# First two experts' token lists from 16 columns of marks, and the first three tiles' result rows gathered in two passes

## What is computed

```python
def hierarchical_moe(xn, w_rg, b_rg, w_re, b_re, w_g, w_u, w_d):
    ...
    g_sel = jnp.argmax(g_logits, axis=-1)
    ...
    top_v, top_i = lax.top_k(e_in, TOP_K)
    top_p = jax.nn.softmax(top_v, axis=-1) * g_w
    expert_idx = (g_sel[:, None] * EXPERTS_PER_GROUP + top_i).reshape(-1)
    ...
    def expert_block(args):
        xb, e = args
        hb = jax.nn.silu(xb @ w_g[e]) * (xb @ w_u[e])
        return hb @ w_d[e]
    ...
    out = jnp.zeros((t, d), xt.dtype).at[token_idx[order]].add(y)
```

## Time and profile before

| | us |
|---|---|
| median of 3 runs | 2050.01 (2047.39 to 2053.05) |
| profiled execution | 2050.37 |
| its span | 2048.6 |
| PE busy | 1976.5 (96%) |
| DVE busy | 992.1 (48%) |
| ACT busy | 558.7 (27%) |
| POOL busy | 416.3 (20%) |

### The profile page before, as it was taken

The page is one execution under the profiler, slowest core; times in us unless marked ns, Lnnn a source line. Parts: engine busy times, 40 slices in busy tenths (PEclk is TensorE's granted clock), DMA queues, the critical chain, the costliest instruction groups (busy, mean ns, idle before and its releaser), DMA issues.

```text
span 2048.6 us, 38041 instructions
## 1 busy us (share of the span) xinstructions
PE 1976.5 (96%) x15458; PEld 1121.0 (55%) x15458; DVE 992.1 (48%) x1739; ACT 558.7 (27%) x1011; POOL 416.3 (20%) x381
## 2 busy tenths in 40 slices
PE   7999999999899999999999999999899999999997
PEld 6476655756434445454445554565566666666653
DVE  3434553455576753586656765444632222222225
ACT  4123231433576221143123421143011111111113
POOL 0304333325252004003000243000011111111113
PEclk9999999999999999999999999999999999999999
DMA  9221230212525012980030411202699999999997
GB/s 398 86 83 37 68 108 26 98 30 84 180 103 175 31 65 74 244 198 1 0 123 11 144 42 56 91 32 75 250 373 399 404 405 412 407 402 413 405 411 273
DMA packets 114572, 369.74 MB, mean 180 GB/s; under 512 B 22920, under 2 KB 58152, under 8 KB 91696
## 3 DMA queue, kind: packets, MB, share of 16 engines
q1 hardware_dynamic: 67520, 280.37, 35.1%
q0 software_dynamic: 20976, 69.23, 11.1%
q10 hardware_dynamic: 25984, 18.91, 2.9%
HBM read 319.17 MB, written 58.07 MB: 184 GB/s over the span
## 4 chain that ended last, share of the span: by engine, by line
PE 86%; DVE 7%; ACT 3%; issue 2%; POOL 1%; DMA 1%; DVEq 0%; ACTq 0%; POOLq 0%; SPq 0%; PEldq 0%
PE bank L760 19%; PE bank L1641 16%; PE bank L753 13%; PE bank L970 9%; PE bank L1651 8%; PE bank L996 2%; PE bank L1056 2%; ACT work L1751 2%; PE bank L1171 1%; PE bank L1632 1%; DVE work L2293 1%; PE bank L828 1%; DVE O L2293 1%; PE bank L1394 1%; PE bank L1164 1%
## 5 line engine op out<-in xcount | busy, mean ns | idle before, releaser
L1751 ACT ACTIVATE work<-bank 128x512 f32<-128x512 f32 (+5 forms) x246 | 123.0, 519 | 327.8 <-PE bank L760 96.1
L1751 ACT ACTIVATE work<-work 128x1024 f32<-128x1024 f32 (+5 forms) x200 | 158.8, 805 | 170.2 <-DVEq L158 114.6
L1751 ACT ACTIVATE HT<-bank 64x256 f32<-64x256 f32 (+1 forms) x150 | 67.8, 452 | 468.1 <-PE bank L1641 303.4
L753 PE MATMUL bank<-slots,HT 128*128 128x512 f32 (+2 forms) x576 | 184.1, 475 | 2.0 <-ACT HT L1751 1.5
L1641 PE MATMUL bank<-slots,HT 128*32 128x256 f32 x3136 | 172.4, 379 | 2.2 <-DVE HT L3152 1.3
L1641 PE MATMUL bank<-work,HT 128*32 128x256 f32 x3072 | 168.7, 379 | 0.0
L3158 DVE TENSOR_TENSOR HT<-HT,bank 64x256 f32<-64x256 f32 x97 | 41.2, 424 | 259.7 <-ACT HT L1751 254.9
L3277 POOL TENSOR_TENSOR work<-work 128x1024 f32<-128x1024 f32 (+1 forms) x64 | 111.9, 1748 | 239.7 <-DVEq L158 160.7
L1641 PEld LDWEIGHTS bank<-slots,HT 128*32 128x32 f32 x3136 | 103.0, 110 | 68.5 <-DMA slots<-in_w_e_up_dram 1.4
L753 PEld LDWEIGHTS bank<-slots,HT 128*128 128x128 f32 x576 | 98.3, 190 | 76.6 <-issue 71.2
L1641 PEld LDWEIGHTS bank<-work,HT 128*32 128x32 f32 x3072 | 101.2, 110 | 64.6
(11 more groups left out here) (356 smaller groups left out, 3114.7 us busy)
## 6 DMA issues: line engine op xcount, KB each, us to landing
slots<-in_w_e_gate_dram SPq DMA_DIRECT2D x34, 1024.0 KB, 9.6
slots<-in_w_e_up_dram SPq DMA_DIRECT2D x34, 1024.0 KB, 12.2
slots<-in_w_e_down_dram SPq DMA_DIRECT2D x17, 2048.0 KB
work<-in_w_e_gate_dram SPq DMA_DIRECT2D x32, 1024.0 KB
work<-in_w_e_up_dram SPq DMA_DIRECT2D x32, 1024.0 KB
work<-in_w_e_down_dram SPq DMA_DIRECT2D x16, 2048.0 KB
y_of_slot<-masks POOLq DMA_DIRECT2D x1, 19712.0 KB, 105.7
slots<-in_w_in_dram SPq DMA_DIRECT2D x8, 2048.0 KB, 8.9
```

Of the source, the lines that this page charges most:

```text
L753: ins = pe.matmul(bank, lhsT, rhs, start=(n == 0), stop=(n == len(pairs) - 1))
L1751: return act.activation(o, i, f, bias=bias, scale=scale, **more)
```

## The change

It does two things. First, the lists of experts 0 and 1 no longer come from the marks of all experts. DVE writes FIRST_MARKS, 16 columns (two experts by eight tiles), scans and hands them to PE ahead of A2. PE makes their ranks alone, then each expert's list in a bank of its own; `index[0]` goes to POOL while index 1 is still open. DVE hears POOL's issue of gather 0, then scans A2; GT, the one-hots OH, PICKED and RANK_OF come after index 1, and the block arithmetic is now `blocks_and_rows()`, behind the first `block_ready`. Dummy products: 3, 1 and 2 where there were 3, 3 and 5, and the last two stand ahead of `emptied()` rather than behind it. Second, POOL gathers the result rows of tiles 0, 1 and 2 twice: a first time ahead of the spare blocks, with all numbers of spare rows out of bounds and so skipped, and a second time after `moe_over` with `spare_id`, in which the regular rows are out of bounds. The readers wait for four transfers of such a tile.

```diff
+        TWICE = 3
         combined = [*((s, 32) for s in dma_in), *((sem(f"combine_rows{i}"), 0) for i in range(4, NT))]
         out_sem = x_in
         YG = [work[:, i * D:(i + 1) * D] for i in range(16)]
...
 
+            def ranks(marks, upto, n):
+
+                bank = ringV.open(pe)[:, 0:n]
+                pe.matmul(bank, const("negtri"), marks, start=True, stop=False)
+                ringV.close(pe.matmul(bank, const("ones"), upto, start=False, stop=True))
+
             hear("dve")
-            n = NT * EXPERTS
-            bank = ringV.open(pe)[:, 0:n]
-            pe.matmul(bank, const("negtri"), A2, start=True, stop=False)
-            ringV.close(pe.matmul(bank, const("ones"), UPTO, start=False, stop=True))
+            ranks(FIRST_MARKS, FIRST_UPTO, 2 * NT)
+            idle_products(banks[0], 1)
+            for e in range(2):
+                bank = ringV.open(pe)[0:CAP, 0:1]
+                for i in range(NT):
+                    at = e * NT + i
+                    if at % MARKED == 0:
+                        pe.wait_ge(rows_marked, at // MARKED + 1)
+                    ins = pe.matmul(bank, ROWS[:, at, :], FIRST_TOKENS[:, at:at + 1], start=(i == 0), stop=(i == NT - 1))
+                ringV.close(ins)
+            hear("dve")
+            ranks(A2, UPTO, NT * EXPERTS)
             bank = ringV.open(pe)[:, 0:EXPERTS]
             ringV.close(pe.matmul(bank, const("ones"), cut(UPTO, EXPERTS)[:, :, NT - 1], start=True, stop=True))
-            idle_products(banks[0], 3)
-            bank = ringV.open(pe)[0:CAP, 0:2]
-            for at in range(2 * NT):
-                if at % MARKED == 0:
-                    pe.wait_ge(rows_marked, at // MARKED + 1)
-                ins = pe.matmul(bank, ROWS[:, at, :], FIRST_TOKENS[:, at, :], start=(at == 0), stop=(at == 2 * NT - 1))
-            ringV.close(ins)
 
             def turn_block(x, last):
                 for half, bank in enumerate(TURN_BANKS):
@@ -1653,8 +1663,8 @@
                                             start=(f == 0), stop=(f == DE // P - 1))
                 ins.then_inc(full, 1)
 
+            idle_products(banks[0], 2)
             emptied()
-            idle_products(banks[0], 5)
             pe.wait_ge(rows_gathered[0], 16)
             turn_block(0, tokens_turned)
             def list_products():
@@ -1721,7 +1731,7 @@
                 residual(n)
             pe.wait_ge(diags_ready, 1)
             for n, i in enumerate(SUMMED):
-                pe.wait_ge(combined[i][0], combined[i][1] + 32)
+                pe.wait_ge(combined[i][0], combined[i][1] + (64 if i < TWICE else 32))
                 for half, bank in enumerate(sum_banks(n)):
                     for x in range(2):
...
@@ -3065,9 +3075,8 @@
             g = LG[:, :, 0:GROUPS]
             e = LG[:, :, GROUPS:].rearrange("p i (g x) -> p i g x", g=GROUPS)
             by_group = "p (i x g) -> p i g x"
-            reduce(R1, g, ALU.max)
-            first_of(OHG, g, R1, GROUPS, RG)
-            tt(GT, g, wide(R1, GROUPS), ALU.subtract)
+            reduce(R3, g, ALU.max)
+            first_of(OHG, g, R3, GROUPS, RG)
             tt(CHOSEN.rearrange(by_group, i=NT, g=GROUPS), e, bcast(OHG.unsqueeze(3), [P, NT, GROUPS, PER_GROUP]), ALU.mult)
             best = cut(BEST, NT)
             reduce(BEST, CHOSEN.rearrange("p (a g) -> p a g", g=GROUPS), ALU.add)
@@ -3077,34 +3086,52 @@
             reduce(R2, best, ALU.max)
             first_of(FIRST[1], best, R2, PER_GROUP, INDEX[:, NT:])
             tt(FIRST[2], FIRST[0], FIRST[1], ALU.add)
+            first = "p (x i) -> p i x"
+            tt(FIRST_MARKS.rearrange(first, x=2), bcast(OHG[:, :, 0:1], [P, NT, 2]), FIRST[2][:, :, 0:2], ALU.mult)
+            line(dve.tensor_tensor_scan(FIRST_UPTO, OF_EXPERT[:, 0:2 * NT], FIRST_MARKS, 0.0, ALU.mult, ALU.add))
+            tell("pe")
+            tt(cut(FIRST_TOKENS, 2), cut(FIRST_MARKS, 2), bcast(const("token").unsqueeze(1), [P, 2, NT]), ALU.mult)
             shape = [P, NT, GROUPS, PER_GROUP]
             tt(A2.rearrange("p (g x i) -> p i g x", g=GROUPS, i=NT), bcast(OHG.unsqueeze(3), shape),
                bcast(FIRST[2].unsqueeze(2), shape), ALU.mult)
+
+            def mark_rows(at, of):
+
+                some, shape = slice(at, at + MARKED), [P, MARKED, CAP]
+                dve.tensor_tensor(ROWS[:, some, :], bcast(const("slot_of_row").unsqueeze(1), shape),
+                                  bcast(of[:, some].unsqueeze(2), shape), ALU.is_equal).then_inc(rows_marked, 1)
+
+            empty(lambda b: dve.tensor_copy(FIRST_RANKS, b[:, 0:2 * NT]))
+            hear("pool")
+            for at in range(0, 2 * NT, MARKED):
+                mark_rows(at, FIRST_RANKS)
+
+            def first_index(x):
+
+                bank = ringV.take(dve)
+                line(dve.tensor_scalar(EMPTY[0:CAP, x:x + 1], bank[0:CAP, 0:1], 0.0, 2.0 * T, ALU.is_equal, ALU.mult))
+                line(dve.scalar_tensor_tensor(out=index[x][0:CAP, :], in0=bank[0:CAP, 0:1], scalar=-1.0,
+                                              in1=EMPTY[0:CAP, x:x + 1], op0=ALU.add, op1=ALU.add), ringV.free)
+                tell("pool")
+
+            first_index(0)
+            hear("pool")
             line(dve.tensor_tensor_scan(UPTO, OF_EXPERT, A2, 0.0, ALU.mult, ALU.add))
             tell("pe")
+            tt(GT, g, wide(R3, GROUPS), ALU.subtract)
+            first_index(1)
             tt(R3, R2, R1, ALU.subtract)
             tell("act")
             for x in range(2):
                 tt(OH[:, x * NT:(x + 1) * NT, :].rearrange("p i (g x) -> p i g x", g=GROUPS), bcast(OHG.unsqueeze(3), shape),
                    bcast(FIRST[x].unsqueeze(2), shape), ALU.mult)
-            ts(RG, RG, float(PER_GROUP), 1024.0 * (PER_GROUP + 1), ALU.mult, ALU.add)
-            tt(cut(INDEX, 2), cut(INDEX, 2), bcast(RG.unsqueeze(1), [P, 2, NT]), ALU.add)
-
-            tt(FIRST_TOKENS.rearrange("p (x i) e -> p x i e", x=2), OH.rearrange("p (x i) e -> p x i e", x=2)[:, :, :, 0:2],
-               bcast(const("token").unsqueeze(1).unsqueeze(3), [P, 2, NT, 2]), ALU.mult)
             shape = [P, 2, NT, EXPERTS]
             four = "p (x i) e -> p x i e"
             empty(lambda b: dve.tensor_tensor(
                 PICKED.rearrange(four, x=2), OH.rearrange(four, x=2),
                 bcast(b[:, 0:NT * EXPERTS].rearrange("p (e i) -> p i e", i=NT).unsqueeze(1), shape), ALU.mult))
             reduce(RANK_OF, PICKED, ALU.add)
-            hear("pool")
-
-            def mark_rows(at, of):
-
-                some, shape = slice(at, at + MARKED), [P, MARKED, CAP]
-                dve.tensor_tensor(ROWS[:, some, :], bcast(const("slot_of_row").unsqueeze(1), shape),
-                                  bcast(of[:, some].unsqueeze(2), shape), ALU.is_equal).then_inc(rows_marked, 1)
+            empty(lambda b: dve.tensor_scalar(SPN, b[:, 0:EXPERTS], 1.0 / TG, BELOW - (CAP + 1 - TG) / TG, ALU.mult, ALU.add))
 
             def mark(at):
 
@@ -3114,34 +3141,27 @@
                 tt(TOKENS[:, some, :], TOKENS[:, some, :], bcast(const("token")[:, i:i + MARKED].unsqueeze(2), shape), ALU.mult)
                 mark_rows(at, ROW_OF)
 
-            for at in range(0, 2 * NT, MARKED):
-                mark_rows(at, RANK_OF)
-            empty(lambda b: dve.tensor_scalar(SPN, b[:, 0:EXPERTS], 1.0 / TG, BELOW - (CAP + 1 - TG) / TG, ALU.mult, ALU.add))
-            bank = ringV.take(dve)
-            line(dve.tensor_scalar(EMPTY[0:CAP, 0:2], bank[0:CAP, 0:2], 0.0, 2.0 * T, ALU.is_equal, ALU.mult))
-            for x in range(2):
-                line(dve.scalar_tensor_tensor(out=index[x][0:CAP, :], in0=bank[0:CAP, x:x + 1], scalar=-1.0,
-                                              in1=EMPTY[0:CAP, x:x + 1], op0=ALU.add, op1=ALU.add), ringV.free if x else None)
-            tell("pool")
-            hear("pool")
-
...
+            def blocks_and_rows():
+
+                ts(RG, RG, float(PER_GROUP), 1024.0 * (PER_GROUP + 1), ALU.mult, ALU.add)
+                tt(cut(INDEX, 2), cut(INDEX, 2), bcast(RG.unsqueeze(1), [P, 2, NT]), ALU.add)
...
@@ -3190,6 +3210,8 @@
                 ts(BEYOND, BLOCK_OF, -float(EXPERTS), 0.0, ALU.add, ALU.max)
                 stt(SLOT, BEYOND, -float(CAP - TG), SLOT, ALU.mult, ALU.add)
                 copy(slot_id[:, :], SLOT)
+                ts(BEYOND, SLOT, float(EXPERTS * CAP), BEYOND_Y, ALU.is_lt, ALU.mult)
+                line(dve.tensor_tensor(spare_id[:, :], SLOT, BEYOND, ALU.add))
                 ts(PIECES, ASSIGNED, const("slot_of_piece"), BEYOND_Y, ALU.is_le, ALU.mult)
                 line(dve.tensor_tensor(piece_list[:, :], PIECES, const("piece_of_y"), ALU.add))
                 dve.sem_inc(routed, 1)
@@ -3216,6 +3238,7 @@
             line(dve.memset(token_list[:, :], 0))
             dve.wait_ge(tokens_turned, 1)
             block_ready(tokens_ready)
+            blocks_and_rows()
             expert(0, 0, first=True)
             expert(0, 1, second=True)
```

(21 more changed lines are left out.)

40 lines of the change are left out of this document (21 added, 19 removed).

## The result

The changed kernel takes 2062.89 us (median of 5 runs, 2058.05 to 2063.33) against 2050.01 (5 runs too, 2047.39 to 2053.05). The ratio, which is estimated from the runs and is not the quotient of the two medians (1.0063), is 1.0052, with a 95% interval of 1.0035 to 1.0069: it is slower by about 0.5%, and its median lies outside the range that was forecast. The medians of all kernels here are of fast runs, and one execution of late_weights (experiment 7) that took 2980.28 us is left out. The profiled execution has a span of 2061.5 us where before it was 2048.6, 12.9 more. Two marks of DVE cut both spans into three parts: the addition of the last tile's logits (128x36), where the routing's chain begins, and the last copy of the loop (128x256, line 3214 before and 3236 after).

The account below looks back on a forecast made before the run. PE's own length bounds the expert loop, leaving the routing ahead and the combination behind to the change. Routing -3.5 us and combination +6 us give +2.5, so 2052.5 us for the median; forecast 2050 to 2055, range 2046.5 to 2059.

Parts of the forecast that it names:

- (b): Routing: the first expert's index told at 1448.4 us, not 1455.1, with PE's eight products half of 2.82 us.
- (d): Routing: the first gather lands 7 us after its issue, at 1456.4, between 1452.9 and 1459.3; by the skill's fit 1453.4.
- (e): Routing: after PE's own ranks and dummies, turning of the first block starts at 1456.6 instead of 1462.52: -5.9 us.
- (f): Routing: PE's low clock slows the first turning (0.8 us) and products (1.5 to 2.5): +2.4 us, bounds 0 and 4.
- (h): Combination: the loop's last scatter lands no sooner than 2.6 us after issue; first-pass gathers start at 2001.3 to 2001.8.
- (j): Combination: PE waits for the spare block's look-ahead gather, so its turn_block starts 8.2 us later.
- (l): Combination: after idling 8 us PE runs the dummies and part of the residuals at 1.2 GHz: +1 to +3 us.
- (k): Combination: PE's 2.94 us of waiting for tile rows goes: +8.2 - 2.9 = +5.3 us for the last sum.
- (n): Combination: the store backlog after the last half tile, 4.4 us to the span's end before, becomes 1.3 us smaller.
- R4: Routing: PE held by emptied() and its dummies until 1459, gain -3, clock takes 2.4; +5.5, 2055.5 us; chance 0.12.
- R5: Every block product until 1465 at half rate, turning at 1456.6: routing -5.9 + 4, combination +8; 2056.1 us, chance 0.08.
- R1: Both low clocks last long, gather shares queue with expert 1's weights: routing -1, combination +8.5; 2057.5 us, chance 0.14.

Follow-up runs that it names:

- late_weights: routing_six with expert 1's upper gate and up rows and down weights (4 MB) loaded only after the first gather has landed; 2044.84 us, ratio 0.9975.
- experiment 7: Expert 1's later weight load in three kernels: late_weights 2044.84 us; the kernel before 2048.28 us; the kernel of experiment 1 2048.61 us.
- kernels 1 and 2: The kernels of experiment 1 (changed kernel without its second part, 2049.02 us) and experiment 2 (kernel before with only the second part, 2060.53 us).
- before_again: The kernel before, unchanged, profiled once more; 2051.23 us.
- Experiments 6 and 7: 6: dummy products added at the routing to experiment 1's kernel, early (routing_six, 2047.89 us) or, separately, late (four for two, 2049.17 us). 7: see experiment 7.
- routing_six: The kernel of experiment 1 with six early dummy products on PE in place of three; 2047.89 us, ratio 0.9991.
- experiment 2: The kernel before with only the change's second part, result rows of tiles 0 to 2 gathered in two passes; 2060.53 us, ratio 1.0057.
- experiment 1: The changed kernel with its second part undone, all result rows gathered once after moe_over; 2049.02 us, ratio 0.9991.
- Experiment 4: The kernel of experiment 2 with the spare block's look-ahead gather issued ahead of the first pass; 2054.58 us, ratio 1.0027.

## Why the prediction was wrong

**Where the 12.9 us went.** +3.45 before the routing, -2.97 in it, +12.42 behind the loop. The first is no work of the change: PE does the same with the lower level granted for a part of the stretches 120 to 140 and 940 to 960 us. PE's rows (busy time, clock, DMA share, GB/s), first before and then after:

```profile
120.00:140.00 20.00, 20.00 (x89) 1.00 0.14 59
940.00:960.00 20.00, 16.10 (x110) 1.00 0.01 1
```

```profile
120.00:140.00 20.00, 20.00 (x81) 0.91 0.16 66
940.00:960.00 20.00, 16.10 (x84) 0.91 0.00 1
```

Each is a loss of 1.7 us. They were also in kernels 1 and 2, and one of them in before_again, so they belong to the execution. The ratio of the times, 10.7 us, is near the sum of the other two parts, 9.5.

**Routing: right in its mechanism, with three sizes off.** (a) The word to PE came 1.2 us sooner, as forecast. (b) The first index came 1.5 us later than I had it: I took the list products at their length of before, 2.82 us, and they ran at half clock. (c) held: the gather started a microsecond after the index. (d) It landed 7.2 us after its issue, 7 forecast, and that agreement is luck. Experiments 6 and 7 show that the weight load decides when it lands: issued at the time I had forecast (10.5 us after the logits; routing_six has 10.8) it takes 8.7 us, and the shorter landing of 2.9 to 4 us that (d) gives beside its 7 is met only when the weights are held back (4.0). So (d) was too short by 1.7 us, and (b) cost nothing in the end. (e) -5.9 us became -4.3, since what PE waited for was this gather and not its own dummies. (f) +2.4 became 1.6, the products alone; the turning was at full clock. (g) cost nothing, as I had it: the list products follow the block's products without a wait. The sum was -3.0 against -3.5. But it was made against one execution of before in which half clock lay on the dummies; over all kernels with the old routing it is 1.7 us, and by the times 1.8.

**Combination: this is what failed.** The wait was named rightly, but PE's turning came 12.8 us later and not 8.2. The letters are the prediction's; the first row counts from the loop's end.

| step | forecast | measured |
|---|---|---|
| (h) first pass begins | 4.6 | 8.0 |
| (i) from there to the look-ahead gather's issue | 8.7 | 9.0 |
| (i) from its issue to the turning | 3.1 | 4.0 |
| (j) turning later by | +8.2 | +12.8 |
| (l) half clock on the turning and the dummies | +2 | +3.5 |
| (k) the rest of PE's row, waits that go | -2.9 | -3.7 |
| (n) from PE's last sum to the end | -1.3 | -0.1 |
| sum of (j) to (n), by unrounded times | +6 | +12.4 |

Step (h) is the main error, 3.4 of the 6.4 us. I gave the last scatter the shortest landing of an indirect transfer, 2.6 us, which was that of a gather with the DMA share at 0.11 (2001 to 2004 us before), and left its bounds at half a microsecond, though the scatters of the same line in the loop took 5.2 to 7.3 us from issue to landing. In the change it took 5.0. I named the wait for ACT's four stores of the same expert but gave it no price: in the change the last of them landed 0.4 us behind the scatter, 6.5 us after its issue. And the first gather's issue followed 1.0 us after that. In the 2 us from the scatter's issue the DMA share is 0.78 at 306 GB/s (the row of 1999 above), so both have other transfers in front of them or beside them. Why they took this long was not taken apart further.

In (l) I took 2 of a range of 1 to 3, and PE was at 0.50 through the turning and nearly all dummies: 0.66 + 2.85 us. The rule of the Trainium skill ("TensorE: Matmul & The Clock Gate", HAM oscillation), that work behind a wait for a transfer starts at the low level, held here, with 0.50 in the row of 2010.

In (n) I counted on a shorter backlog of stores; it was shorter (2.6 us from the end of the last half tile to the end of the span, not 4.4), but DVE's last half tile began 4.0 us behind PE's last sum in place of 2.3, because DVE had become as long a chain as PE. Here the prediction was at odds with itself: among its signs it put about 8 us from the last sum to the end, which is what was measured (8.0; 8.15 before), and that leaves nothing for the -1.3 of its sum.

**Rivals.** R2 (the end costs nothing) and R3 (the clock stays up in both places) fall with experiment 2 and with the 0.50 in the row of 2010. R4 and R5 have 6 and 8 us at the combination, where 12.4 were measured; the 0.6 and 1.9 us that they leave to the routing are both within what experiment 1 allows (0.2 to 3.7 us), but R4's hold, PE's own dummies, was not what held PE, and R5's half clock under all products to 1465 (+4) was 1.6. R1's condition was met: the first gather landed 19.2 us after the logits, which is 1458.2 on the clock of before. It named the slower side, with 0.14, and put 2.5 us of excess into each place; the excess was all in the combination, in the wait for the scatter and the stores. Even R1 with its 2057.5, and the range's end at 2059, lie below the median.

Experiment 4 adds what the sum had hidden under (k): without PE's wait the kernel is still 5.5 us slower, with 5.60 us of waiting for rows behind the gathers of the second pass. In neither of the two orders that were tried did the second part win.

## What to carry to other kernels

A transfer that is issued earlier need not land earlier: here one issued 1.2 us sooner landed no sooner while 6 MB of weights were under way. See what has been issued and not landed, and try to hold back loads that are not needed yet. Work that is put into an engine's idle time must be set against what stands behind it on that engine, down to waits of no use such as the last look-ahead block, and its start must be priced with every transfer that it waits for, at the landing time that the same line has under load. When PE's idle time is shortened or lengthened, price its next work at both clock levels, and take the baseline from more than one profile if the effect sought is of that size.

## What was not expected of the hardware

At the routing the half clock came when PE was back at work: in the change PE idled from 1445.53 to 1448.45, its clock was at 1.00 until 1450 and then at 0.51 for 10 us in which PE was busy for 9.75. In the long wait of the combination, from 2005.65 on, it fell within the wait. Executions differ in where such stretches fall, two profiles of the kernel before too (1.00 and 0.91 over 120 to 140 us), 1.7 us each. The last scatter of the loop landed 4.1 to 5.0 us after its issue, while the look-ahead gather, in before with the DMA share at 0.11, took 2.6. Gathers with a bound on their rows were issued one each 1.31 us, those without it one each 1.25; one of which nearly all rows are skipped held POOL as long (1.00 us) as a full one.
